# Pair attention on one Trainium2 core: two parts of a short pair turned into one PSUM bank, read by one copy, and one reciprocal for each pair

## The chip, the core and the metric

The kernel runs on one core of a Trainium2 chip. The time is the device time of one launch in microseconds (us). PE is TensorE's matmul unit, PEld its weight load, DVE is VectorE, ACT is ScalarE, POOL is GpSimd and SP is SyncE.

## What is computed

The reference passes 512 tokens of width 1024 through three transformer blocks. Each has gated linear layers and mixers, and each has softmax attention over short sequences. The change touches only those attentions. Cut to what matters, the three are:

```python
# first block: for each of 16 heads, three branches (compressed keys, selected blocks, window)
p_cmp = masked_softmax(q @ k_cmp.T * scale - slope * distance, seen)      # 31 compressed keys
o = g0 * (p_cmp @ v_cmp) + g1 * (softmax(...) @ v_sel) + g2 * (softmax(...) @ v_win)
# second block: sparse heads, and differential heads
o_sparse = softmax(q @ k.T + bias + penalty) @ v
o_diff = (attn_map(q1, k1) - lam * attn_map(q2, k2)) @ v
# third block: six heads with a forgetting term
logits = q @ k.T * scale + (c[q] - c[k]);  o = softmax(causal(logits)) @ v
```

## The kernel before, in words

Matmuls of the linear layers ("dense" below, lines L719 to L721, three products for one block of 128 input features) are interleaved with the attention by `run_lanes`: each engine has one program for each lane, and `paced` fixes by hand the order in which all five engines step through the lanes. An engine works strictly in that order.

The attention lane is `PairAttend`. Its queries come in tiles of 128 tokens, and an item is a pair of parts (two heads, or the two maps of a differential head) for one query tile t and one kind of key. A part has t + 1 blocks of 128 keys, or one block of 31 for the compressed keys. For item i:

- PE computes the scores of both parts (`scores`, L933; in the third block also L939).
- DVE adds the bias and takes the row minimum (`lowest`, L1007), part by part.
- ACT takes the exponential with its row sum (`exponential`, L1040), part by part.
- DVE inverts the two row sums (`invert`, L987) and multiplies the rows by them and by the gate (`share`, L1023; L1017 and L1019 for joined items, whose two parts become one matrix).
- PE transposes the weights, block by block, into the PSUM tile `turn`, which is one bank of 512 columns (`turn`, L950). ACT copies that bank into `probs_t` (`read_turned`, L1053). The bank is single, so the next turn waits for the copy (`turned_read`).
- PE multiplies with the values (`weigh`, L964) into `out_acc`; ACT copies that out at the end of a group (L1066).

The lane is pipelined by slots. In slot s PE does the scores of item s, the turn of part 0 of item s - 3, the weighing of item s - 4, and then the turn of part 1 of item s - 3. A dense step may follow. ACT in that slot does: copy of part 0, exponential of part 0 of item s, copy of part 1, exponential of part 1. DVE does the minima of item s, then the inversion and the multiplication of item s - 1.

There are 138 items: 96 in the first attention (8 head pairs, 4 query tiles, 3 kinds; the two-deep score buffers are `score_sets=2`), 30 in the second (10 sparse and 20 joined) and 12 in the third. I call the items of one head pair in the first attention A0, A1, A2 (t = 0), B0, B1, B2 (t = 1), C0 to C2 and D0 to D2, where kind 0 is the compressed one with 31 keys. In the first attention POOL also builds the bias tables of the next head pair in the meantime.

## Time and profile before

| | |
|---|---|
| median of 3 runs | 3330.89 us (3327.81 to 3335.61) |
| the profiled execution | 3334.52 us, its span 3332.8 us |
| PE busy, over the span | 3032.6 us, 91% |
| ACT, DVE, POOL busy | 35%, 34%, 37% |
| granted PE clock, mean | 0.943 of full speed |
| first attention | about 229 to 493 us of the span |
| second attention | about 1633 to 1790 us |
| third attention | about 2745 to 2826 us |

Busy PE time is the time covered by its matmuls from start to modelled end. Since matmuls are pipelined, what a step costs PE is better read as the time from its first start to the start of the next step. All such intervals below are differences of two start times in the timeline.

### The profile page before, as it was taken

The page shows a single profiled execution, that of the slowest core. Times are in us where ns is not written, and L with a number is a line of the kernel's source. Part 1 is how long each engine was busy: PE and PEld are TensorE (multiplying, and loading weights), DVE is VectorE, ACT ScalarE, POOL GpSimd, SP SyncE. Part 2 cuts the span into 40 slices and gives each one's busy share as a digit, 9 for nine tenths or more (in the row PEclk, how much of TensorE's full clock was granted, in tenths as well). Part 3 has the DMA queues.
Part 4 walks back from the last instruction along what each step waited for, and adds up shares of the span by engine and source line. Part 5 has one row for each costly group of instructions (what it writes and reads, how often), then busy time and mean ns, then how long its engine had stood idle before and what let it go on. Part 6 is the DMA issues. An engine that isn't in the chain of part 4 may idle for free. (4 is left out here: it accounts for less than half of the span.)

```text
span 3332.8 us, 44710 instructions
## 1 busy us (share of the span) xinstructions
PE 3032.6 (91%) x17513; PEld 2486.4 (75%) x17513; DVE 1123.0 (34%) x2511; ACT 1152.6 (35%) x2136; POOL 1240.2 (37%) x599
## 2 busy tenths in 40 slices
PE   4879999998999959999999989999897899989998
PEld 3765557887877757766787989999786756868877
DVE  4116651111132031664353432220364732322210
ACT  3237763222243223343354422221233345423221
POOL 3232214454344412122122535544354422535543
PEclk8889999999999977999899989999898999989999
DMA  6320002232232202012122412223222222413322
GB/s 225 109 63 20 20 15 87 89 101 82 89 108 83 89 26 69 26 45 64 64 78 81 160 58 88 88 88 97 69 79 91 73 69 78 163 63 95 101 88 95
DMA packets 83502, 272.96 MB, mean 82 GB/s; under 512 B 9879, under 2 KB 10135, under 8 KB 83204
## 3 DMA queue, kind: packets, MB, share of 16 engines
q1 hardware_dynamic: 80956, 267.62, 25.3%
q10 hardware_dynamic: 2376, 3.00, 0.3%
q8 instruction: 116, 1.90, 0.2%
q14 instruction: 54, 0.44, 0.0%
HBM read 255.68 MB, written 14.90 MB: 81 GB/s over the span
## 5 line engine op out<-in xcount | busy, mean ns | idle before, releaser
L157 POOL TENSOR_TENSOR weights_lo<-weights_raw,weights_hi 128x1024 fp32r<-128x1024 f32 x415 | 1009.1, 2438 | 1370.5 <-ACT weights_hi L149 1370.3
L149 ACT ACTIVATE weights_hi<-weights_raw 128x1024 fp32r<-128x1024 f32 x415 | 436.8, 1056 | 859.0 <-PE acc L721 347.5
L195 PE MATMUL acc<-h_hi,weights_hi 128*128 128x264 f32 (+1 forms) x1616 | 546.9, 338 | 44.2 <-PEq L87 36.2
L719 PE MATMUL acc<-h_hi,weights_hi 128*128 128x512 f32 (+1 forms) x1336 | 509.1, 381 | 50.4 <-PEq L513 18.9
L196 PE MATMUL acc<-h_lo,weights_hi 128*128 128x264 f32 (+1 forms) x1616 | 545.3, 337 | 0.0
L197 PE MATMUL acc<-h_hi,weights_lo 128*128 128x264 f32 (+1 forms) x1616 | 545.1, 337 | 0.0
L720 PE MATMUL acc<-h_lo,weights_hi 128*128 128x512 f32 (+1 forms) x1336 | 477.6, 358 | 0.0
L721 PE MATMUL acc<-h_hi,weights_lo 128*128 128x512 f32 (+1 forms) x1336 | 476.8, 357 | 0.0
L719 PEld LDWEIGHTS acc<-h_hi,weights_hi 128*128 128x128 f32 x1336 | 262.6, 197 | 139.8 <-issue 108.8
L195 PEld LDWEIGHTS acc<-h_hi,weights_hi 128*128 128x128 f32 x1616 | 307.9, 191 | 76.9 <-issue 46.3
L196 PEld LDWEIGHTS acc<-h_lo,weights_hi 128*128 128x128 f32 x1616 | 308.1, 191 | 30.8
L197 PEld LDWEIGHTS acc<-h_hi,weights_lo 128*128 128x128 f32 x1616 | 307.9, 191 | 30.9
L721 PEld LDWEIGHTS acc<-h_hi,weights_lo 128*128 128x128 f32 x1336 | 262.8, 197 | 33.5
L720 PEld LDWEIGHTS acc<-h_lo,weights_hi 128*128 128x128 f32 x1336 | 263.5, 197 | 28.6 <-issue 0.9
L195 PE MATMUL acc<-hidden_hi,weights_hi 128*128 128x264 f32 (+1 forms) x528 | 170.7, 323 | 15.0 <-PEq L87 15.0
L196 PE MATMUL acc<-hidden_lo,weights_hi 128*128 128x264 f32 (+1 forms) x528 | 170.5, 323 | 0.0
L197 PE MATMUL acc<-hidden_hi,weights_lo 128*128 128x264 f32 (+1 forms) x528 | 170.2, 322 | 0.0
L1053 ACT ACTIVATE probs_t<-turn 31x128 f32<-31x128 f32 (+5 forms) x256 | 99.0, 387 | 156.3 <-PE turn L950 152.7
L1040 ACT ACTIVATE probs<-probs,low 128x31 f32<-128x31 f32 (+5 forms) x276 | 139.2, 505 | 31.1 <-DVE low L1007 30.8
L1148 POOL TENSOR_TENSOR hidden_lo<-full,hidden_hi 128x528 f32 (+3 forms) x44 | 57.7, 1311 | 236.5 <-DVE hidden_hi L1204 236.5
L1194 DVE TENSOR_SCALAR conv<-gate_pad,vec 128x528 f32<-128x528 f32 (+1 forms) x44 | 24.2, 551 | 319.1 <-ACT gate_pad L1177 319.1
L950 PE MATMUL turn<-const,probs 128*128 128x128 f32 (+3 forms) x564 | 111.5, 286 | 20.7 <-ACT probs_t L1053 13.6
(392 smaller groups left out, 4815.4 us busy)
## 6 DMA issues: line engine op xcount, KB each, us to landing
weights_raw<-in_stream SPq DMA_DIRECT2D x415, 512.0 KB, 3.6
weight_ring<-in_w_ada SPq DMA_DIRECT2D x24, 512.0 KB, 12.2
gates<-gate_tiles SPq DMA_DIRECT2D x24, 264.0 KB, 4.4
gate<-gates SPq DMA_DIRECT2D x8, 792.0 KB, 5.8
gates<-gate_tiles SPq DMA_DIRECT2D x24, 256.0 KB, 4.3
gate<-gates SPq DMA_DIRECT2D x8, 768.0 KB, 5.6
flipped<-bias_rows SPq DMA_DIRECT2D x8, 320.0 KB, 4.6
x<-in_x ACTq DMA_DIRECT2D x1, 2048.0 KB, 21.5
```

The source lines that it names most:

```text
L149: act.activation(self.hi[:, at % CUT, :], self.raw[:, at % RAW, :], ACT.Copy).then_inc(self.hi_done, 1)
L157: pool.tensor_tensor(self.lo[:, at % CUT, :], self.raw[:, at % RAW, :], self.hi[:, at % CUT, :].bitcast(F32), ALU.subtract).then_inc(self. ...
L195: pe.matmul(accs[half], w_hi, x_hi[:, cols], start=start, stop=False)
L196: pe.matmul(accs[half], w_hi, x_lo[:, cols], start=False, stop=False)
L197: last = pe.matmul(accs[half], w_lo, x_hi[:, cols], start=False, stop=stop)
L719: pe.matmul(out, left[0], right[0], start=start, stop=False)
L720: pe.matmul(out, left[0], right[1], start=False, stop=False)
L721: return pe.matmul(out, left[1], right[0], start=False, stop=stop)
L950: last = pe.transpose(self.turn[0:kb, b * part.nq:(b + 1) * part.nq], self.probs[0:part.nq, self.place(i, m), c:c + kb], self.k.ident[0:pa ...
L1040: act.activation(rows, rows, ACT.Exp, bias=self.low[0:part.nq, at, :], scale=-1.0, accum_out=self.row_sum[0:part.nq, at, :]).then_inc(self ...
L1053: last = act.activation(to[0:rows, 0:len(full) * part.nq], self.turn[0:rows, 0:len(full) * part.nq], ACT.Copy)
L1148: pool.tensor_tensor(tile_at(hidden.lo, i, n, w), full[:, u], tile_at(hidden.hi, i, n, w).bitcast(F32), ALU.subtract).then_inc(rest_done, 1)
```

## The change

A pair that is not joined, whose parts together fill at most 512 columns and whose blocks are all of one height, is turned at once: the transposes of both parts go one behind the other into the same bank, part 1 in the columns behind part 0, with one semaphore count, and one ACT instruction copies both (its output jumps by 512 columns between the parts). PE then weighs without a second turn behind it. Such pairs are those with one or two blocks: A and B items and all kind 0 items in the first attention (64 of 96), 4 of 30 in the second, 6 of 12 in the third, 74 in all. Longer pairs and joined ones go as before. In all 138 items DVE inverts both row sums in one instruction, which waits for both exponentials.

```diff
+        self.at_once = [not joined and 2 * len(a.blocks) * a.nq <= 512 and len(set(kb for _, kb in a.blocks)) == 1 for a, _, joined in self.items]
+        turns = [1 if joined or once else 2 for (_, _, joined), once in zip(self.items, self.at_once)]
...
         def turn(i, m):
             part, n = self.items[i][m], self.turns_to[i] + m
-            pe.wait_ge(self.weights_ready, n + 1)
+            pe.wait_ge(self.weights_ready, self.weights_to[i + 1] if self.at_once[i] else self.weights_to[i] + m + 1)
             if n >= 1:
 
                 pe.wait_ge(self.turned_read, n)
-            for b, (c, kb) in enumerate(part.blocks):
-                last = pe.transpose(self.turn[0:kb, b * part.nq:(b + 1) * part.nq], self.probs[0:part.nq, self.place(i, m), c:c + kb],
-                                    self.k.ident[0:part.nq, 0:part.nq])
+            for both in range(2 if self.at_once[i] else 1):
+                for b, (c, kb) in enumerate(part.blocks):
+                    col = (both * len(part.blocks) + b) * part.nq
+                    last = pe.transpose(self.turn[0:kb, col:col + part.nq], self.probs[0:part.nq, self.place(i, m + both), c:c + kb],
+                                        self.k.ident[0:part.nq, 0:part.nq])
             last.then_inc(self.turned, 1)
...
         def invert(i):
-            for m in range(2):
-                nq, at = self.items[i][m].nq, self.place(i, m)
-                dve.wait_ge(self.exp_done, 2 * i + m + 1)
-                dve.reciprocal(self.row_inv[0:nq, at, :], self.row_sum[0:nq, at, :]).then_inc(self.row_inverted, 1)
+            nq, at = self.items[i][0].nq, self.place(i, 0)
+            dve.wait_ge(self.exp_done, 2 * i + 2)
+            dve.reciprocal(self.row_inv[0:nq, at:at + 2, 0], self.row_sum[0:nq, at:at + 2, 0]).then_inc(self.row_inverted, 1)
...
             rows = part.blocks[0][1]
+            if self.at_once[i]:
+                cols = len(part.blocks) * part.nq
+                act.activation(self.probs_t[0:rows, 2 * (i % 2):2 * (i % 2) + 2, 0:cols], self.turn[0:rows, 0:2 * cols].rearrange("p (m c) -> p m c", m=2),
+                               ACT.Copy).then_inc(self.turned_read, 1)
+                return
...
-            if turns is not None and not self.items[turns][2]:
+            if turns is not None and self.two_turns(turns):
                 read_turned(turns, 1)
```

On PE, in the first attention in the third head pair, this is the order before, from the scores of a B1 item to those of a C0 item; the turned items are A1 and A2, one block each.

```order
L933 MATMUL scores<-keys_t,q 128x256 x2
L950 MATMUL turn<-const,probs 128x128
L964 MATMUL out_acc<-probs_t,v_cmp 64x128 x2
L950 MATMUL turn<-const,probs 128x128
L719 MATMUL acc<-h_hi,weights_hi 128x512
L720 MATMUL acc<-h_lo,weights_hi 128x512
L721 MATMUL acc<-h_hi,weights_lo 128x512
L933 MATMUL scores<-keys_t,q 128x256 x2
L950 MATMUL turn<-const,probs 128x128
L964 MATMUL out_acc<-probs_t,v_tok 64x128 x2
L950 MATMUL turn<-const,probs 128x128
L933 MATMUL scores<-k_cmp,q 128x31 x2
```

The same place in the changed kernel, whose lines are shifted (L940 for L933, L959 for L950, L973 for L964):

```order
L940 MATMUL scores<-keys_t,q 128x256 x2
L959 MATMUL turn<-const,probs 128x128 x2
L973 MATMUL out_acc<-probs_t,v_cmp 64x128 x2
L719 MATMUL acc<-h_hi,weights_hi 128x512
L720 MATMUL acc<-h_lo,weights_hi 128x512
L721 MATMUL acc<-h_hi,weights_lo 128x512
L940 MATMUL scores<-keys_t,q 128x256 x2
L959 MATMUL turn<-const,probs 128x128 x2
L973 MATMUL out_acc<-probs_t,v_tok 64x128 x2
L940 MATMUL scores<-k_cmp,q 128x31 x2
```

The second transpose moved from behind the weighing to in front of it; nothing else on PE moved, and there are as many matmuls as before.

On ACT, where item A0 is turned, and just before it the last turn of D2 is copied, the order before is this (`probs_t<-turn` is the copy, `q<-out_acc` the output of a group):

```order
L1053 ACTIVATE probs_t<-turn 128x512
L1040 ACTIVATE probs,row_sum<-probs,low 128x128
L1053 ACTIVATE probs_t<-turn 31x128
L1040 ACTIVATE probs,row_sum<-probs,low 128x31
L1053 ACTIVATE probs_t<-turn 31x128
L1040 ACTIVATE probs,row_sum<-probs,low 128x31
L1066 ACTIVATE q<-out_acc 128x128
```

And in the changed kernel, with the two items behind it:

```order
L1066 ACTIVATE probs_t<-turn 128x512
L1048 ACTIVATE probs,row_sum<-probs,low 128x128
L1060 ACTIVATE probs_t<-turn 31x2x128
L1048 ACTIVATE probs,row_sum<-probs,low 128x31 x2
L1079 ACTIVATE q<-out_acc 128x128
L1060 ACTIVATE probs_t<-turn 128x2x128
L1048 ACTIVATE probs,row_sum<-probs,low 128x256 x2
L149 ACTIVATE weights_hi<-weights_raw 128x1024
```

The copy that stood between the two exponentials is gone; one copy of twice the columns stands ahead of both.

## Rows read from the trace of the kernel before

**Rows 1.** Busy us and count of each engine, clock, DMA: first attention

```profile
229.00:493.00 264.00, 236.30 (x1729) 140.80 (x1730) 164.16 (x769) 177.97 (x626) 59.89 (x40) 0.97 0.07 21
```

**Rows 2.** Timeline of PE, third head pair: start, us, instruction, idle before

```profile
303.67 0.41 PE L933 MATMUL scores<-k_cmp,q 64*128 64x31 f32 x4
304.01 0.30 PE L950 MATMUL turn<-const,probs 128*31 128x128 f32 x1
304.24 1.09 PE L964 MATMUL out_acc<-probs_t,v_tok 128*64 128x128 f32 x16
305.26 0.30 PE L950 MATMUL turn<-const,probs 128*31 128x128 f32 x1
305.49 0.70 PE L933 MATMUL scores<-keys_t,q 64*128 64x256 f32 x4
306.12 0.33 PE L950 MATMUL turn<-const,probs 128*128 128x128 f32 x1
306.47 0.43 PE L964 MATMUL out_acc<-probs_t,v_cmp 31*64 31x128 f32 x4
306.91 0.30 PE L950 MATMUL turn<-const,probs 128*128 128x128 f32 x1
306.97 0.48 PE L719 MATMUL acc<-h_hi,weights_hi 128*128 128x512 f32 x1
...
308.48 0.33 PE L950 MATMUL turn<-const,probs 128*128 128x128 f32 x1
308.74 0.44 PE L964 MATMUL out_acc<-probs_t,v_tok 128*64 128x128 f32 x4
309.27 0.30 PE L950 MATMUL turn<-const,probs 128*128 128x128 f32 x1
309.50 0.41 PE L933 MATMUL scores<-k_cmp,q 64*128 64x31 f32 x4
310.03 0.27 PE L950 MATMUL turn<-const,probs 128*31 128x128 f32 x1
310.23 0.44 PE L964 MATMUL out_acc<-probs_t,v_tok 128*64 128x128 f32 x4
310.75 0.27 PE L950 MATMUL turn<-const,probs 128*31 128x128 f32 x1
310.77 0.47 PE L719 MATMUL acc<-h_hi,weights_hi 128*128 128x512 f32 x1
```

**Rows 3.** Timeline of PE, third attention, an item with two blocks

```profile
2770.55 0.44 PE L950 MATMUL turn<-const,probs 128*128 128x128 f32 x2
2770.92 0.44 PE L964 MATMUL out_acc<-probs_t,v_tok 128*64 128x128 f32 x4
2771.55 0.41 PE L950 MATMUL turn<-const,probs 128*128 128x128 f32 x2 [0.20 <-ACT probs_t L1053]
2771.72 0.48 PE L719 MATMUL acc<-h_hi,weights_hi 128*128 128x512 f32 x1
```

**Rows 4.** Timeline of PE, second attention, dense work right behind a weighing

```profile
1650.03 0.45 PE L964 MATMUL out_acc<-probs_t,v_tok 128*64 128x128 f32 x4
1650.41 0.39 PE L719 MATMUL acc<-h_hi,weights_hi 128*128 128x264 f32 x1
```

**Rows 5.** Timeline of PE, two turns with idle time ahead

```profile
241.54 0.39 PE L950 MATMUL turn<-const,probs 128*31 128x128 f32 x1 [1.14 <-ACT probs_t L1053]
...
312.73 0.41 PE L950 MATMUL turn<-const,probs 128*128 128x128 f32 x2 [0.18 <-DVE probs L1023]
```

**Rows 6.** Timeline of ACT: the copy of B0's second part

```profile
312.34 0.25 ACT L1053 ACTIVATE probs_t<-turn 31x128 f32<-31x128 f32 x1
```

**Rows 7.** Timeline of DVE: both multiplications of B1

```profile
309.53 2.35 DVE L1023 TENSOR_SCALAR probs<-probs,row_inv,gates 128x256 f32<-128x256 f32 x2
```

**Rows 8.** Groups by line and shape, first attention: count, busy us, mean ns, idle

```profile
L987 DVE RECIPROCAL row_inv<-row_sum 128x1 f32<-128x1 f32 x192 | 22.7, 152 | 2.5 <-ACT probs L1040 2.3
...
L1053 ACT ACTIVATE probs_t<-turn 128x512 f32<-128x512 f32 x32 | 19.1, 597 | 18.5 <-PE turn L950 18.5
```

More of the change, by code:

```diff
@@ L881, in __init__ @@
         self.last_of = [max(i for i in range(N) if self.of[i][0] == g) for g in range(len(groups))]
-        turns = [1 if joined else 2 for _, _, joined in self.items]
+        self.at_once = [not joined and 2 * len(a.blocks) * a.nq <= 512 and len(set(kb for _, kb in a.blocks)) == 1 for a, _, joined in self.items]
+        turns = [1 if joined or once else 2 for (_, _, joined), once in zip(self.items, self.at_once)]
+        weights = [1 if joined else 2 for _, _, joined in self.items]
+        self.weights_to = [sum(weights[:i]) for i in range(N + 1)]
         self.turns_to = [sum(turns[:i]) for i in range(N + 1)]
@@ L900, in __init__, with two_turns @@
         self.weights = [item[0].nk for item in self.items] + [P] * (self.WEIGH + 1)
+    def two_turns(self, i):
+        return self.turns_to[i + 1] - self.turns_to[i] == 2
     def place(self, i, m):
@@ L1013, in share @@
             inv = [self.row_inv[0:part.nq, self.place(i, m), :] for m, part in ((0, a), (1, b))]
-            dve.wait_ge(self.row_inverted, 2 * i + 2)
+            dve.wait_ge(self.row_inverted, i + 1)
             if joined:
@@ L1070, in act @@
                 exponential(s, 0)
-            if turns is not None and not self.items[turns][2]:
+            if turns is not None and self.two_turns(turns):
                 read_turned(turns, 1)
```

## The prediction, made before the changed kernel ran

> **What bounds the kernel now.** I looked first at the busy shares: PE is busy 91% of the span, no other engine over 37%. Then at the three attention stretches alone. In the first, the busiest beside PE is ACT with 178 of 264 us, then DVE with 164, and PE has 236 [rows 1]. So ACT and DVE could follow a somewhat faster PE, and the question is what each slot costs PE. Busy time does not tell this, because a transpose that is "busy" for 0.30 us lets the next instruction start after 0.06 or after 0.23 us. I therefore read starts in PE's timeline. The reader should see there that a slot is a chain of small steps with little named idle time, yet every step that has to wait for a semaphore begins late. A turn of one block followed by another such step takes 0.23 us (305.26 to 305.49), 0.20 with 31 keys (310.03 to 310.23). One followed by dense work takes 0.06 or 0.02 us (306.91 to 306.97, 310.75 to 310.77) [rows 2]. The second thing to see is a round trip. From the start of part 0's turn to the start of part 1's it is 306.12 to 306.91 = 0.79 us and 308.48 to 309.27 = 0.79 us, with only two short products between them; for two blocks it is 2770.55 to 2771.55 = 1.00 us, and there 0.20 us of it shows as idle, ended by the copy [rows 2, 3]. The one bank has to be copied by ACT before part 1 can go in. Where the weighing is long, as behind D2 (304.24 to 305.26 = 1.02 us), it hides the copy.
>
> **The change, part by part.**
>
> The weighing without a round trip in it. Where nothing is turned behind it, a weighing of one block takes 1650.03 to 1650.41 = 0.38 us [rows 4], against 0.44 to 0.53 us in rows 2 (306.47 to 306.91, 308.74 to 309.27). Four blocks take 1.02, so each further block is (1.02 - 0.38) / 3 = 0.21: two blocks 0.59, three 0.81. No row shows a weighing with scores right behind it; it could be as cheap as 0.38 or pay once more the 0.17 us by which a gated step behind a turn (0.23) exceeds an ungated one (0.06). I take 0.38, because the weighing is followed in rows 2 by a gated turn and there, with 1.02 us for four blocks, no such surcharge is visible. The other end is 0.17 us in each of the 22 slots without dense work, 4 us.
>
> The joint turn. Two transposes in a row take 0.37 us (2770.55 to 2770.92) [rows 3], one takes 0.26 (308.48 to 308.74) [rows 2]: one more costs 0.11. With 31 keys I take 0.23 + 0.11 = 0.34, with two blocks (four transposes) 0.37 + 0.22 = 0.59.
>
> Now slot by slot, turn + weighing + turn before, and joint turn + weighing after. The counts are those of the eight head pairs, whose rows repeat; "dense" says that dense work comes right behind.
> - A0, weighing four blocks: before 0.23 + 1.02 + 0.23 = 1.48, after 0.34 + 1.02 = 1.36. Saves 0.12, three times. With dense behind, the second turn cost only about 0.05 and the slot loses about 0.08, four times. C0 and D0 have the same form with two or three blocks weighed: save 0.12 six times, lose 0.08 nine times. Together 9 x 0.12 - 13 x 0.08 = 0.
> - A1 and A2: before 0.26 + 0.53 + 0.23 = 1.02, after 0.37 + 0.38 = 0.75. Saves 0.27 eight times. With dense 0.35 + 0.44 + 0.06 = 0.85, saves 0.10, eight times. Sum 3.0 us.
> - B0, weighing A2: before 0.20 + 0.52 + 0.02 = 0.74 with dense, after 0.72: 0.1 us over six. The two without dense wait longer for the copy and I give them 0.4 each, 0.8. But B0's first turn has to wait for the copy of A2's second part: the 31-key scores ahead of it last 309.50 to 310.03 = 0.53, against 303.67 to 304.01 = 0.34. After the change the weighing (0.38) and the scores (0.34) lie behind A2's turn (0.37), 1.09 us, over the round trip of 1.00. The 0.19 goes, six times 1.1. Sum 2.0.
> - B1: before as in rows 3, 0.37 + 0.63 + 0.17 = 1.17, after 0.59 + 0.38 = 0.97, eight times 0.20 = 1.6. And the 0.18 us idle ahead of B1's first turn [rows 5]. The row names DVE, but B0's second copy ends 312.34 + 0.25 = 312.59 [rows 6], so that is what it waits for; that copy stood behind an exponential, which stood behind DVE's slow multiplication (309.53 to 311.88) [rows 7]. After the change the copy stands ahead of both exponentials. Five head pairs show this idle time, 0.9 us.
> - B2, weighing two blocks: with dense 1.17 before and 0.59 + 0.59 = 1.18 after, nothing; three times without dense the second turn costs 0.34 and not 0.17: 0.5 us.
> - The very first pair: its second turn sat idle for 1.14 us behind the copy, because ACT was still doing exponentials [rows 5]. That idle time goes: 1.1 us.
>
> First attention: 0 + 3.0 + 2.0 + 2.5 + 0.5 + 1.1 = 9.1 us. The second attention has two A and two B items with PE's time in the same form: about 0.5 for the idle time of its first pair, 0.1, 0.3 and 0: 0.9. The third has three and three: 0.5 + 0.1 + 0.1 + 0.2 + 0 + 0 = 0.9. These four smaller figures are estimates by the same three rows. Sum 10.9 us.
>
> What it costs on the engines behind. The joint copy starts one or two transposes later and has twice the columns. It is hidden by weighing and scores, 0.72 us at the least, as computed for B0; the margin there is only 0.09. ACT itself: in slot A2 it has one copy and two exponentials of 256 columns, and PE needs 0.63 + 0.75 = 1.38 us without dense work. ACT may be behind PE there by a few tenths, and a rounding of weights also falls in this place. B1's joint turn waits for both multiplications. They ended at 311.88, the turn began at 312.73, 0.85 us later; PE will come some 0.5 us earlier by then. I deduct 0 to 3 us for such lateness and take 0.4, because both margins are positive in the rows.
>
> The reciprocals. 138 instructions of about 0.15 us leave DVE [rows 8], 21 us. DVE's multiplications are ready 0.85 us or more before PE wants them, so this is worth nothing on PE's path; if that cover were gone it would be worth up to 0.15 us in an item, and in such items it would reduce the lateness above. The joint one waits for the second exponential; the multiplications waited for that anyway.
>
> The sum: 10.9 - 0.4 = 10.5 us. Against the profiled execution, 3334.5 - 10.5 = 3324.0. That execution lay 3.6 us above the median of the three runs, so the median becomes 3330.9 - 10.5 = 3320.4 us.
>
> The Trainium skill speaks against this part of the change. Perfetto Trace Analysis, section Optimizing Scalar/DVE Operations, says that where ACT or DVE are not saturated but cause bubbles on another engine, breaking instructions up may let work finish sooner; here the instruction is made larger, with ACT at 178 of 264 us. By that rule this would cost time, the second rival below. The rows side with the merger, since the bubble they show is the number of round trips through one bank and not the length of a copy.
>
> **The rivals.**
> 1. Gain given back by ACT and DVE, so that nothing can be measured. For it: the margins 0.09 and 0.85 us, and slots of 1.38 us in which ACT must fit two exponentials. Against it: ACT and DVE have a third of the stretch free. If the surcharge of 0.17 us behind the weighing holds (4 us) and lateness costs 3, then 10.9 - 7 = 4 us remain: 3327.
> 2. The late half, on the slower side. What comes next on the bank waits for the whole joint copy. A 512-column copy takes 0.60 us [rows 8], and it can start only after four transposes. If it were exposed in each of the 74 slots by 0.25 us (an estimate: the copy's added half 0.21, and the added transposes partly), it would cost 18 us against 11 gained: 3338. It decides where exposure is over 11 / 74 = 0.15 us in every slot. Against it: the cover is 0.72 us or more, and 1.6 us with dense work.
> 3. More is gained: the same removed round trip also lets scores and exponentials go earlier, and the remaining waits for the bank in C and D items shrink. Idle times of the kind shown stand before other turns too. I bound it by doubling the two waits priced for B0 and B1, 2 us, and by 0.15 us of DVE lead in 32 short items where it is slowest, 5 us: 3314.
> 4. The change does not do what it says: excluded by the order, which shows the joint turn and copy.
>
> **How the numbers follow.** Forecast (gain of 7 to 14 us) 0.66; rival 1 (gain under 7, about nothing) 0.20; rival 3 (over 14) 0.10; rival 2 0.04. No change means within 0.2%, 6.7 us, about what a measurement here can tell. Faster: forecast and rival 3, 0.76, and a little of rival 1's upper end does not count: 0.76. Same 0.20, slower 0.04. The range runs from rival 3's 3314 to just beyond rival 1, 3328; it leaves out rival 2 and the tails.
>
> **What would show it.** Right: in the same slots, a joint turn then a weighing of 0.38 us and scores or dense work at once; A1 and A2 slots shorter by 0.1 to 0.3 us; the first attention about 9 us shorter, the second and third about 1 us each, everything else as it was; ACT's wait for turns shorter. Wrong: idle time ahead of the joint turns, put down to ACT's copy or DVE's multiplication; a weighing followed by scores that takes 0.55; or a different granted clock in stretches that the change does not touch.

## The result, and the profile after

The changed kernel took 3314.28 us (median of 6 runs, 3309.45 to 3318.38), the kernel before in the same session 3331.89 us (6 runs). The ratio is 0.9943, interval 0.9927 to 0.996: 13 to 24 us less, where 10.5 us less was forecast. Two repeats in later sessions gave 0.9971 (0.9959 to 0.9983) and 0.9947 (0.9928 to 0.9965), so 10 to 19 us is what one should carry. The forecast of 3320.4 us had a range of 3314 to 3328, a gain of 3 to 17 us on the 3330.9 us it started from; the 17.6 us measured here lie just beyond it. The direction and most steps were right. But some two fifths of this saving came from where the prediction had nothing, and one of its terms, B1's, did not come at all.

The profiled execution took 3315.77 us with a span of 3314.1 us, PE's mean granted clock 0.945 (before: span 3332.8 us, 0.943). First the view by windows of the first attention, with the columns of [rows 1]:

```profile
229.00:487.00 258.00, 235.90 (x1728) 140.70 (x1727) 158.41 (x672) 168.57 (x561) 59.85 (x40) 0.95 0.07 21
```

The two windows differ by 6 us because they are cut at whole microseconds; from the first scores to the end of the last weighing it is 262.2 us before and 257.4 after, at a lower clock (0.95 against 0.97), with 97 DVE and 65 ACT instructions fewer. Now PE's timeline in the third head pair, which answers to [rows 2]:

```profile
303.48 0.41 PE L940 MATMUL scores<-k_cmp,q 64*128 64x31 f32 x4
303.82 0.41 PE L959 MATMUL turn<-const,probs 128*31 128x128 f32 x2
304.16 1.09 PE L973 MATMUL out_acc<-probs_t,v_tok 128*64 128x128 f32 x16
305.18 0.70 PE L940 MATMUL scores<-keys_t,q 64*128 64x256 f32 x4
305.82 0.44 PE L959 MATMUL turn<-const,probs 128*128 128x128 f32 x2
306.19 0.44 PE L973 MATMUL out_acc<-probs_t,v_cmp 31*64 31x128 f32 x4
306.55 0.50 PE L719 MATMUL acc<-h_hi,weights_hi 128*128 128x512 f32 x1
...
307.45 0.70 PE L940 MATMUL scores<-keys_t,q 64*128 64x256 f32 x4
308.08 0.44 PE L959 MATMUL turn<-const,probs 128*128 128x128 f32 x2
308.45 0.44 PE L973 MATMUL out_acc<-probs_t,v_tok 128*64 128x128 f32 x4
308.82 0.41 PE L940 MATMUL scores<-k_cmp,q 64*128 64x31 f32 x4
309.16 0.41 PE L959 MATMUL turn<-const,probs 128*31 128x128 f32 x2
309.49 0.44 PE L973 MATMUL out_acc<-probs_t,v_tok 128*64 128x128 f32 x4
309.86 0.50 PE L719 MATMUL acc<-h_hi,weights_hi 128*128 128x512 f32 x1
...
310.75 0.92 PE L940 MATMUL scores<-keys_t,q 64*128 64x384 f32 x4
311.60 0.65 PE L959 MATMUL turn<-const,probs 128*128 128x128 f32 x4
312.69 0.43 PE L973 MATMUL out_acc<-probs_t,v_cmp 31*64 31x128 f32 x4 [0.44 <-ACT q L1079]
313.06 0.50 PE L719 MATMUL acc<-h_hi,weights_hi 128*128 128x512 f32 x1
```

Subtract neighbouring starts. A joint turn takes 308.08 to 308.45 = 0.37 us, with 31 keys 0.34. A weighing of one block takes 308.45 to 308.82 = 0.37 us although gated scores follow it; the surcharge of 0.17 us that was open in the prediction does not exist. From the scores that open one slot to those of the next, the slots in which A1, A2 and B0 are turned went from 2.36, 1.65 and 2.14 us (in the trace of [rows 2]) to 2.27, 1.37 and 1.93. The wrong place is the third from the end: the weighing behind B1's turn of four sat idle for 0.44 us, and from the turn to the weighing it is 1.09 us and not 0.59. ACT's timeline shows why:

```profile
309.82 0.36 ACT L1060 ACTIVATE probs_t<-turn 31x256 f32<-31x256 f32 x1
311.67 0.32 ACT L1048 ACTIVATE probs<-probs,low 128x31 f32<-128x31 f32 x1 [1.49 <-DVE low L1015]
311.89 0.19 ACT L1048 ACTIVATION_READ_ACCUMULATOR probs<-probs,low 128x1 f32 x1
311.99 0.30 ACT L1048 ACTIVATE probs<-probs,low 128x31 f32<-128x31 f32 x1
312.20 0.19 ACT L1048 ACTIVATION_READ_ACCUMULATOR probs<-probs,low 128x1 f32 x1
312.29 0.26 ACT L1079 ACTIVATE q<-out_acc 128x128 f32<-128x128 f32 x1
```

The weighing opens a group, so `out_acc` must have been read. The copy that reads it (L1079) stands behind the exponentials of C0, and these waited for DVE's minima. The same queue was there in the kernel before:

```profile
312.80 0.25 ACT L1066 ACTIVATE q<-out_acc 128x128 f32<-128x128 f32 x1
```

There the copy ended at 313.05 us and the weighing started at 313.19; in the changed kernel the copy ended at 312.55 and the weighing started at 312.69. Both start 0.14 us behind the copy's end. Before, the turn ahead began late, so that only 0.09 us of this showed (312.73 to 313.19 = 0.46 us from turn to weighing, against 0.37 for such a pair of transposes elsewhere). DVE was late, as its timeline in the changed kernel shows, since B1's multiplications took 2.46 us:

```profile
308.87 0.16 DVE L995 RECIPROCAL row_inv<-row_sum 128x2 f32<-128x2 f32 x1
309.07 2.46 DVE L1031 TENSOR_SCALAR probs<-probs,row_inv,gates 128x256 f32<-128x256 f32 x2
311.45 0.17 DVE L1015 CUSTOM_DVE_ANT_0 probs<-scores,alibi_cmp 128x31 f32<-128x31 f32 x1
...
311.86 0.73 DVE L1031 TENSOR_SCALAR probs<-probs,row_inv,gates 128x256 f32<-128x256 f32 x2
```

The same two multiplications took 0.73 us three microseconds later. Beside the slow ones POOL ran this:

```profile
308.68 2.37 POOL L157 TENSOR_TENSOR weights_lo<-weights_raw,weights_hi 128x1024 fp32r<-128x1024 f32 x1 [8.34 <-ACT weights_hi L149]
```

In the whole trace of the changed kernel, each of the 38 multiplications of 128x256 with no POOL instruction beside it took 0.35 to 0.49 us; the eight with this subtraction beside them for over nine tenths of their time took 1.58 to 2.55 us. No run takes the subtraction away, so that it is the cause is likely but not shown.

To size all terms I added up the slots of head pairs 2 to 7 (from the first scores of the second pair to the first scores of the eighth; PE at full clock in both traces) by the item turned in them. "Forecast" is three quarters of the prediction's figure, as these are six of eight pairs:

| us saved in six head pairs | forecast | changed kernel |
|---|---|---|
| A0, C0, D0 and D1 | 0 | 1.4 |
| A1, A2 | 2.3 | 2.3 |
| B0 | 1.5 | 1.6 |
| B1 | 1.9 | -0.2 |
| B2 | 0.4 | 0.5 |
| sum | 6.0 | 5.5 |

These six pairs took 186.88 us before and 181.39 after. In B1's row, the five slots with the wait went from 3.11 to 3.20 us each; the sixth, where nothing waits, gained its 0.2 us as forecast.

### The profile page after: what moved, and what is told of

It is laid out like the page before. It is cut to its first block and busy times, and to the rows that moved or that the text cites. A ratio compares the mean times of both kernels' runs of the same rounds, so it can differ in the third digit from the quotient of the medians.

```text
span 3314.1 us, 44424 instructions
## 1 busy us (share of the span) xinstructions
PE 3021.7 (91%) x17513; PEld 2478.6 (75%) x17513; DVE 1115.1 (34%) x2373; ACT 1141.6 (34%) x2062; POOL 1240.1 (37%) x599
## 5 line engine op out<-in xcount | busy, mean ns | idle before, releaser
L195 PEld LDWEIGHTS acc<-hidden_hi,weights_hi 128*128 128x128 f32 x528 | 100.8, 191 | 22.8 <-issue 15.7
L959 PE MATMUL turn<-const,probs 128*128 128x128 f32 (+3 forms) x564 | 98.1, 284 | 12.3 <-ACT probs_t L1066 11.3
```

The costliest lines, as they stand in the source:

```text
L195: pe.matmul(accs[half], w_hi, x_hi[:, cols], start=start, stop=False)
L959: last = pe.transpose(self.turn[0:kb, col:col + part.nq], self.probs[0:part.nq, self.place(i, m + both), c:c + kb], self.k.ident[0:part.nq ...
```

## Where the rest came from: the clock and a transfer

Outside the attentions, the largest difference between the two first executions lies between the first and the second attention, 1140.2 us before and 1132.8 after. There `BiasTables` turns eight tables on PE, each fetched by SP into one of two buffers (`flipped`). PE's timeline of the kernel before, where the fifth table is turned:

```profile
1594.46 1.53 PE L2329 MATMUL turn<-flipped,const 128*128 128x320 f32 x4 [1.25 <-DMA flipped<-bias_rows]
```

and of the changed kernel:

```profile
1587.38 1.34 PE L2342 MATMUL turn<-flipped,const 128*128 128x320 f32 x4
```

The wait of 1.25 us is gone. Windows of 22 us from just ahead of these turns, before and then changed (the eighth figure, behind POOL's, is the granted clock):

```profile
1590.00:1612.00 22.00, 20.75 (x81) 15.62 (x79) 3.82 (x5) 3.09 (x5) 2.34 (x1) 0.69 0.37 122
```

```profile
1583.00:1605.00 22.00, 21.91 (x120) 16.82 (x119) 5.34 (x7) 5.35 (x10) 3.97 (x2) 1.00 0.37 130
```

PE is busy in both, but did 81 matmuls in the one and 120 in the other: before, PE ran at half clock (1.2 GHz instead of 2.4) for 13.7 us from 1595.5 us on.

The second such place is the second attention itself. It took 154.6 us before, 17.1 of them at half clock, and 148.7 after, 5.3 of them at half clock; less half of that time, both are 146.0 us. So these 5.9 us are clock too. The repeats below had 17.1 and 17.1 us of half clock there before, and 11.5 and 5.4 in the changed kernel. But two kernels with the joint turn (B1 in two halves, and two copies) had 17.4 us each, with no wait of over 0.47 us for a table. What this stretch follows is not shown.

Half clock is all over this program: in the records of granted clock it adds up to 382.2 us before and 365.0 after. While PE is busy, a microsecond at half clock does about half a microsecond's work (81 matmuls against 120 above), so span less half of that time is a rough measure of the work itself. I call it the levelled span: 3141.7 us before, 3131.6 after.

## The experiments

**The kernel before, again,** unchanged (twice).

> The kernel before once more, unchanged. Two theories share the 17.6 us. Slots: the changed slots alone are worth about 5 us in the first attention and 2 in the others; the other 10 or so are TensorE clock, since the changed kernel spent less time at half clock around 1595 to 1650 us of the span. Chance: that clock difference is luck of the two profiled executions. If chance, this profile may show the half clock around 1595 us gone, and its time within 0.1% of the others all the same. If it belongs to the kernel, the half-clock stretches of about 14 us at 1595 us and of about 17 us at 1633 us are here again. Ratio 1.000 in both cases.

> The kernel before a third time. Theory: span less half of the half-clock time 3141 to 3143 us again; the 1.25 us for which TensorE waits for the fifth table's rows may come out anywhere between 0.6 and 1.3 us with the transfer's own time, and the half clock of 13.7 us behind it is there if the wait is 1.2 us or more, as in three executions, and not if it is 1.0 or less. Rival (the stretch of 13.7 us at 1595 us belongs to the kernel before whatever the wait): there at any wait.

**The changed kernel, again,** unchanged (twice).

> The changed kernel itself once more. Theory (the gain over what the slots give is TensorE's clock around 1590 to 1650 us, and belongs to the kernel and not to a single execution): the half-clock stretches come again at 1617.8 us (6.8 us long) and 1768 us, none at 1590 to 1600 us, and the time is 3314.3 plus or minus 3. Rival (the clock's pattern differs from one execution to the next): a half-clock stretch of some 13.7 us at 1590 to 1600 us, and a span of 3320 us.

> The changed kernel a third time. Theory (the change saves 10 to 12 us of work, and what a session measures beyond or below it is how long TensorE ran at half clock): span less half of its half-clock time 3130 to 3132 us as in the first two executions (3131.6 and 3130.4), against 3142 before; the half-clock time may be anything from 350 to 382 us, the span accordingly 3305 to 3322. Rival (the changed kernel belongs to a lower half-clock time, and all of the 18 us is its own): half-clock time again 365 plus or minus 3 us and the time 3314 plus or minus 2, 14 us or more below the kernel before.

| execution | us, ratio to before | span | half clock | levelled span |
|---|---|---|---|---|
| before, first | | 3332.8 | 382.2 | 3141.7 |
| before, second | 3330.03, 0.9999 (0.9987 to 1.0011) | 3330.0 | 375.4 | 3142.2 |
| before, third | 3328.86, 0.9999 (0.9987 to 1.0012) | 3325.4 | 361.7 | 3144.5 |
| changed, first | 3314.28, 0.9943 (0.9927 to 0.996) | 3314.1 | 365.0 | 3131.6 |
| changed, second | 3316.15, 0.9971 (0.9959 to 0.9983) | 3312.9 | 365.1 | 3130.4 |
| changed, third | 3309.54, 0.9947 (0.9928 to 0.9965) | 3308.1 | 351.6 | 3132.3 |

The mean levelled span falls by 3142.8 - 3131.4 = 11.4 us, with 2 to 3 us between executions of one kernel. The stretch behind the fifth table's turn came again in both repeats of the kernel before, for 13.7 and 6.8 us, and in none of the changed kernel's. The mean half-clock time falls by 12.5 us, from 373.1 to 360.6, worth 6.3. Within one kernel it varies by 14 to 20 us from one execution to the next, so three of each can't size this part well. Against the rival of the last expectation the changed kernel's half-clock time was not again 365 but 351.6 us.

**The reciprocal alone,** joined, in the kernel before:

```diff
-            for m in range(2):
-                nq, at = self.items[i][m].nq, self.place(i, m)
-                dve.wait_ge(self.exp_done, 2 * i + m + 1)
-                dve.reciprocal(self.row_inv[0:nq, at, :], self.row_sum[0:nq, at, :]).then_inc(self.row_inverted, 1)
+            nq, at = self.items[i][0].nq, self.place(i, 0)
+            dve.wait_ge(self.exp_done, 2 * i + 2)
+            dve.reciprocal(self.row_inv[0:nq, at:at + 2, 0], self.row_sum[0:nq, at:at + 2, 0]).then_inc(self.row_inverted, 1)
```

> The joint reciprocal alone, everywhere; turns as before. Prediction's step: nothing, because the multiplications are ready 0.85 us or more before PE wants them (ratio 1.000, within 0.001). Rival: the DVE chain behind B1 (multiplications slowed to 1.2 us each) sets the start of the weighing there, and then one reciprocal less on DVE is worth 0.1 us in five head pairs, 0.5 us, still within the noise; over 3 us would mean that DVE holds PE back in many items.

3330.04 us, ratio 0.9996 (0.9985 to 1.0008). Head pairs 2 to 7 took 186.83 us against 186.88 before.

**The joint turn alone,** the reverse of that edit in the changed kernel.

> The changed kernel with the two reciprocals of an item apart again, so the joint turn and copy alone. Theory (the reciprocal lies beside PE's path): the first attention stays at 258.3 plus or minus 0.5 us and the time at that of the changed kernel, 3314 to 3317. Rival (the shorter DVE chain made part of the gain that the joint turn got): the slots in which DVE is slow grow by up to 0.15 us each, 3318 to 3322.

3319.99 us, ratio 0.9973 (0.9963 to 0.9983). The time is nearer to the rival's, the trace is not: head pairs 2 to 7 took 181.37 us against 181.39 in the changed kernel. The reciprocal is worth nothing on PE's path in either direction. The levelled span was 3127.3 us here, 3 us below the changed kernel's lowest with the same slots, so that measure is good to some 5 us and no better.

**The joint turn in the first attention only,** and **in the second and third only** (both with the joint reciprocal). The edit is a flag in one line, set to False for the other attentions:

```diff
-        self.at_once = [not joined and 2 * len(a.blocks) * a.nq <= 512
+        self.at_once = [once and not joined and 2 * len(a.blocks) * a.nq <= 512
```

> The joint turn only in the first attention, the joint reciprocal everywhere. Slots theory: 5 to 6 us from the first attention. If the clock part comes from how the first attention shifts what follows, 15 us or more (ratio 0.9955 or less); if it comes from the second attention's own start, 5 to 7 us (ratio 0.998 to 0.9985).

> The joint turn only in the second and third attention, the joint reciprocal everywhere. Slots theory: about 2 us if the clock part does not come with it (ratio 0.9994), 8 to 12 us if the removed idle time at the start of the second attention is what brings the clock up sooner (ratio 0.9965 to 0.9975).

First only: 3318.77 us, 0.996 (0.9947 to 0.9973); head pairs 2 to 7 in 181.40 us. Late only: 3325.89 us, 0.9986 (0.9976 to 0.9996); the third attention in 78.12 us against 79.13 before, which are the 0.9 us of the prediction and 0.1 more. First only, whose ratio means 9 to 18 us, came nearer in time to the expectation for the clock than to the 5 to 7 us of the slots; by levelled spans (3136.8 and 3141.2 us) the two are worth 6.0 and 1.6 us, close to the slots' figures.

**ScalarE's output copy earlier.** In the changed kernel, the group's output is copied right behind the turned copy of the slot of its weighing:

```diff
-            done = s - self.WEIGH - 1
-            if done >= 0 and self.of[done][2]:
+            done = s - self.WEIGH
+            if turns is not None:
+                read_turned(turns, 0)
+            if 0 <= done < N and self.of[done][2]:
...
-            if turns is not None:
-                read_turned(turns, 0)
```

> The changed kernel, with ScalarE's copy of the group output moved from the slot behind the weighing of D0 (behind the exponentials of C0) to right behind the turned copy of the same slot. Theory (B1's slot lost its gain to a chain that reaches back from the weighing of B0 over the output copy to VectorE): the weighing of B0 no longer waits 0.44 us for L1079 in five head pairs, B1's slot falls from 3.20 to about 2.75 us in each of them, the first attention from 258.5 to some 256.3 us, and the time by 2.0 to 2.5 us below the changed kernel's 3314.3: 3312. Rival (ScalarE's copy, now ahead of the exponentials, waits for a weighing of one to three blocks and holds the exponentials back): the weighing still waits, for the exponentials or for VectorE's multiplications, and the time is 3314 to 3318.

3312.45 us, ratio 0.9962 (0.9948 to 0.9976), beside 0.9971 for the changed kernel in the same session. The intervals overlap; the trace decides. PE's timeline at the place of the 0.44 us:

```profile
307.24 0.92 PE L940 MATMUL scores<-keys_t,q 64*128 64x384 f32 x4
308.08 0.66 PE L959 MATMUL turn<-const,probs 128*128 128x128 f32 x4
308.67 0.43 PE L973 MATMUL out_acc<-probs_t,v_cmp 31*64 31x128 f32 x4
309.03 0.50 PE L719 MATMUL acc<-h_hi,weights_hi 128*128 128x512 f32 x1
```

and ACT's, where the output copy (L1081) now stands ahead of the exponentials that still wait for DVE:

```profile
306.30 0.36 ACT L1060 ACTIVATE probs_t<-turn 31x256 f32<-31x256 f32 x1
306.57 0.25 ACT L1081 ACTIVATE q<-out_acc 128x128 f32<-128x128 f32 x1
308.15 0.32 ACT L1048 ACTIVATE probs<-probs,low 128x31 f32<-128x31 f32 x1 [1.33 <-DVE low L1015]
```

Turn to weighing is 0.59 us, as the prediction had it, and B1's slot 2.69 us against 3.19 (3.11 before). Head pairs 2 to 7 took 178.86 us, 2.5 less than in the changed kernel, and B1's line of the table becomes 2.3 us saved where 1.9 were forecast. So the chain over the output copy is shown to be what ate that term.

**B1 in two halves again** (`at_once` false for the eight B1 items), the rest as in the changed kernel.

> The changed kernel, where in the first attention the eight B1 items are turned in two halves as before. Theory (the joint turn gained nothing in them, since the weighing of B0 then stands waiting for ScalarE's output copy): their slots go from 3.20 to 3.1 to 3.3 us, the first attention stays within 1 us of 258.4, the time within 1.5 us of the changed kernel's. Rival (my own step in the prediction, 2.5 us for B1): the first attention 2.5 us longer, 260.9.

3318.07 us, ratio 0.9966 (0.9953 to 0.998). B1's slot was 3.36 to 3.38 us against 3.19, head pairs 2 to 7 took 182.45 us: 1.1 us more in six pairs, 1.4 in eight. My theory was too strong. The weighing waits there too, 0.65 us by the trace, but the joint turn does save its 0.18 us. The slot is slower than the 3.11 us of the kernel before, with the same two turns. My reading is that the earlier steps have become faster and PE arrives sooner at a wait that ends at ACT's time; this is argued from the trace and has no run of its own.

**The joint turn with two copies,** one right behind the other, one count.

```diff
-                act.activation(self.probs_t[0:rows, 2 * (i % 2):2 * (i % 2) + 2, 0:cols], self.turn[0:rows, 0:2 * cols].rearrange("p (m c) -> p m c", m=2),
-                               ACT.Copy).then_inc(self.turned_read, 1)
+                for both in range(2):
+                    last = act.activation(self.probs_t[0:rows, 2 * (i % 2) + both, 0:cols], self.turn[0:rows, both * cols:(both + 1) * cols], ACT.Copy)
+                last.then_inc(self.turned_read, 1)
```

> The changed kernel with the joint turn, but ScalarE copies its two halves with two instructions one right behind the other, and counts once, behind the second. Theory (what is gained is PE's round trip between the two turns; how many instructions ScalarE has for the copy matters only where PE waits for it): at most 0.1 us more in each of the five B1 slots that already wait, the first attention 258.3 to 259.5, the time within 2 us of the changed kernel's. Rival (the one instruction is what gains): each copy costs ScalarE some 0.2 us more in 74 slots, the first attention grows by 4 us or more, 3319 to 3322.

3314.7 us, ratio 0.9957 (0.9944 to 0.997). Head pairs 2 to 7 took 181.64 us, 0.25 more than with one instruction. Two copies of 128x256 take 0.64 us together, the single one of 128x512 0.58. The gain belongs to PE's program, with one round trip through the bank in place of two.

**The tables' transfers one slot earlier,** with three buffers, in the kernel before:

```diff
-            if head >= 2:
-                sp.wait_ge(self.turned, head - 1)
+            if head >= 3:
+                sp.wait_ge(self.turned, head - 2)
...
-            sp.dma_start(self.flipped[:, head % 2, :], src).then_inc(self.table_in[head % 2], 16)
-            yield
+            sp.dma_start(self.flipped[:, head % 3, :], src).then_inc(self.table_in[head % 3], 16)
+            if head >= 1:
+                yield
```

> The kernel before, with three buffers for the tables' flipped rows in place of two and each of their transfers issued one slot earlier, so that TensorE does not wait for them. Theory (TensorE's halved clock from 1595.5 us on for 13.7 us follows the 1.25 us for which it waited for the transfer of the fifth table): the waits of turn<-flipped for the transfer, 4.6 us in all, go to under 1 us, the half clock at 1595 us is gone, and the time falls by 6.8 us for the clock and up to 4 us for the waits: 3320 (3317 to 3324). Rival 1 (the clock is halved there for another reason): the half clock stays and only the waits go, 3326 to 3328. Rival 2 (what matters is the total time of idle PE before the second attention's start): the stretch moves to 1625 to 1635 us and is longer, no change of over 3 us.

3322.48 us (11 runs), ratio 0.9989 (0.998 to 0.9998), the median 5.5 us below that of the kernel before in its session, by the interval 1 to 7 us less. The levelled span was 3141.6 us against the mean of 3142.8. No turn of a table waits for its transfer, and the window shows no half clock:

```profile
1590.00:1612.00 22.00, 22.00 (x119) 16.93 (x118) 5.35 (x7) 6.01 (x10) 4.74 (x2) 1.00 0.29 92
```

**The fifth table late,** fetched twice in a row (SP waits for the first transfer), in the changed kernel and in the kernel before, and **the sixth late** in the changed kernel:

```diff
+            if head == 4:
+                sp.dma_start(self.flipped[:, 2, :], src).then_inc(self.first_in, 16)
+                sp.wait_ge(self.first_in, 16)
```

> The changed kernel, with the flipped rows of the fifth table fetched twice, the second time after the first has landed, so that TensorE waits for them at about 1587 us as the kernel before did at 1594 us (that one transfer more is 0.33 MB). Theory (a wait of over a microsecond there brings the halved clock): TensorE waits 1 to 4 us ahead of that table's turn, a half-clock stretch of some 13.7 us follows within a few us, and the time is 3314.3 plus the wait plus 6.8: 3322 to 3325. Rival (the clock does not answer to this wait): the time rises by the wait alone, 3315 to 3318, and the half-clock stretches stay as they were.

> The kernel before with the flipped rows of the fifth table fetched twice, so that TensorE's wait there is 1.25 us plus some 3 us. Theory (a wait of over a microsecond brings the half clock): a half-clock stretch begins within 2 us of that wait's end; its length is open, 13.7 us as in the kernel before or 3.4 us as in the changed kernel with the same edit; the time rises by 3 us and the difference of the stretches. Rival (the stretch has nothing to do with the wait): it begins at 1595.5 us as before, wherever the wait ends.

> The changed kernel with the sixth table's rows fetched twice, so that TensorE waits some 3 us there and not at the fifth. Theory (the wait brings the half clock): the stretch of 3.4 us or more moves to that wait, some 6 us later than with the fifth table; the wait is about 3 us and the span less half of the half-clock time rises by it, to 3134 to 3136. Rival (the half clock came by chance at the fifth): no stretch begins within 3 us of the wait's end.

Changed kernel, fifth late: 3322.0 us, 0.9985 (0.9975 to 0.9995), about 6 us above the changed kernel in its session. The time came as expected, the stretch did not: 3.4 us of half clock from 1589.6 us on, and not 13.7. The wait of 3.1 us and half of that stretch make 4.8. Before, fifth late: 3332.54 us, 1.0013 (1.0001 to 1.0025). Its stretch began at 1594.6 us, 2.2 us ahead of the wait's end and 0.3 to 1.4 us from where it began in the kernel before (1594.9 to 1596.0), so this run does not part the theory from its rival. Sixth late: 3314.05 us, 0.9954 (0.9938 to 0.997), where the sixth turn waited only 0.18 us, so the edit did not make the wait it was meant to. But the second turn waited 1.20 us there, on a transfer that the edit does not touch. PE's rows for these waits, in this order:

```profile
1590.13 2.50 PE L2346 MATMUL turn<-flipped,const 128*128 128x320 f32 x4 [3.11 <-DMA flipped<-bias_rows]
```

```profile
1596.76 2.50 PE L2333 MATMUL turn<-flipped,const 128*128 128x320 f32 x4 [4.57 <-DMA flipped<-bias_rows]
```

```profile
1566.10 1.34 PE L2346 MATMUL turn<-flipped,const 128*128 128x320 f32 x4 [1.20 <-DMA flipped<-bias_rows]
```

All profiled executions with such a wait, over all kernels here (half clock that begins within 4 us of the wait's end):

| longest table waits, us | half clock behind it, us |
|---|---|
| 1.25, 1.33, 1.24 (before, before again, late only) | 13.7 each |
| 1.12 (before, third) | 6.8 |
| 4.57 (before, fifth late) | 6.8, begun within the wait |
| 3.11 (changed, fifth late) | 3.4, begun within the wait |
| 1.20 (changed, sixth late) | 3.4 |
| 0.99 (reciprocal alone), 0.94 | none |
| 0.96 twice (changed again; changed, fifth late) | 3.4 once, none once |
| 0.76 and less (in all the others) | none |

Each of the seven table waits of 1.12 us or more had half clock with it, and of the shorter ones only one had. With the two runs that moved the wait (tables earlier: stretch gone; changed kernel, fifth late: stretch there), that ties the stretch to the wait at this place. It is no rule for other waits. In the kernel before, two waits of PE for ACT stand in the same region, with no half clock in them or within 4 us behind them:

```profile
1569.64 1.07 PE L816 MATMUL sums<-sq,const 128*24 128x264 f32 x4 [1.32 <-ACT sq L804]
...
1578.10 1.07 PE L816 MATMUL sums<-sq,const 128*24 128x264 f32 x4 [1.33 <-ACT sq L804]
```

In that whole execution PE was idle for 1.1 to 2.0 us, at full clock, 21 times; half clock began within or up to 4 us behind 10 of them. That a longer wait brings a longer stretch is refuted: the 4.57 us brought 6.8 and the 1.25 us 13.7.

**Both edits together** in the changed kernel, the earlier output copy and the earlier tables.

> The changed kernel with both edits: ScalarE's output copy right behind the turned copy, and three buffers and earlier transfers for the tables' rows. Theory: the output copy is worth the 2.5 us of slots and the 2 to 4 us of first pair and clock that it gave alone; the tables' transfers have only 0.4 us of waiting left to remove, so they add 0 to 1 us, unless a half-clock stretch goes with them: 3309 to 3313, and a span of 3306 to 3309. Rival (the earlier transfers are worth as much here as in the kernel before, 5 us): 3306 or less.

3313.17 us, ratio 0.9953 (0.994 to 0.9966). Head pairs 2 to 7 in 178.86 us and a levelled span of 3124.3 us, the lowest of all, but with 382.2 us of half clock in that execution, so that its span of 3315.4 us missed the expected 3306 to 3309. Levelled spans of kernels with the changed kernel's work scatter from 3127.3 (joint turn alone) to 3132.3 us, so 3 to 8 us are gained by this measure, and by its time it is not told apart from the changed kernel. I would keep both edits, on the evidence of slots and waits.

## Why the prediction was right in most steps and wrong in the number

Two steps failed. Inside the sum it was B1's: the prediction took a wait for gone that only moved on by one instruction. What carried the time out of its range was "everything else as it was", a term put at nothing without a reason: about 6.3 us of clock and 1.4 us of waits for tables came on top.

The sum of the work, 10.5 us, looks as if it held beside the 11.4 us of the levelled spans. That is in part luck. At equal half clock the first attention, from the first scores to the end of the last weighing, took 264.3 us before (third execution, 23.9 us of half clock) and 257.4 in the changed kernel (first execution, 23.8), 6.9 us less where 9.1 were forecast. The third gave 0.9 us, the second 0 to 0.7, so the attentions gave about 8 us and not 10.5. The 11.4 also hold the 1.4 us of table waits, which the prediction did not have; the 1 to 2 us that are left lie within the scatter of that measure. Step by step:

- *The weighing without a round trip, the joint turn:* right to 0.01 us (0.37, 0.59, 0.81 and 1.02 us for one to four blocks; 0.37, 0.34 and 0.59 for the turns). The value taken, no surcharge, was right.
- *A1 and A2, B0, B2:* right, 4.3 us in six pairs against 4.1.
- *A0, C0, D0 = 0:* too low by 1.4 us in six pairs, D1 with them. The prices were right: 0.12 us saved without dense work, 0.07 to 0.09 lost with it. But in three pairs the C0 slot saved 0.19 us instead, since its turn had waited for the copy of B2's second part (the line below) and no longer did; by B0's step the prediction could have listed this too. These are 0.8 of the 1.4. The same kind of wait ahead of D1's turn gave 0.3 (from the scores of D1's slot to its turn 0.51 us before, 0.42 after). The rest is that these six pairs have fewer slots with dense work than all eight.

```profile
379.60 0.27 PE L950 MATMUL turn<-const,probs 128*31 128x128 f32 x1 [0.22 <-ACT probs_t L1053]
```

- *"After the change the copy stands ahead of both exponentials. Five head pairs show this idle time, 0.9 us", and the 1.6 us beside it:* the failed step of the sum. The idle time ahead of B1's turn did go. But the prediction asked only what the turn waits for, not what the weighing right behind it waits for. Since PE came sooner, it met the output copy, 0.44 us in the same five pairs, behind the same slow multiplications. A removed wait moved by one instruction: each of these slots grew by 0.09 us where a gain of 0.38 was forecast. With the output copy moved ahead, B1 gave 2.3 us in six pairs.
- *The first pair, 1.1 us:* the slot of its A0 fell from 3.05 to 1.93 us, as forecast, though 0.30 of the 1.14 us idle are left ahead of the joint turn, now for DVE. The whole pair took 35.48 us before and 36.94 after, with more half clock in it (the stretch at 228.6 us lasted 23.9 us, against 20.5 at 226.7), so this term can't be read from the two first executions. At about equal half clock in the pair (23 to 24.4 us) it took 37.3 to 37.7 us in six executions with the turns apart and 36.6 to 36.9 in six with the joint turn, some 0.8 us less.
- *Second and third attention, 0.9 each:* right for the third, which fell from 79.1 to 78.2 us at equal half clock (3.4 us). For the second it is open. At 17.1 to 17.4 us of half clock it fell from 154.6 to 153.9 us (B1 in halves, two copies); at 13.3 to 13.6 us it took 153.6 with the turns apart (tables earlier) and 153.3 to 153.4 with the joint turn (output copy earlier, both edits), and also 153.4 in the first-only kernel, where the second attention is as before.
- *Lateness 0.4 us and "everything else as it was":* the second half failed, and it is this step that put the time out of its range. Here are about 6 us of clock and 1.4 us of waits for tables (1.9 us before, 0.5 after, means of three, and part of the 11.4). How much of the clock belongs to the change stays open, since it varies as much between executions of one kernel. The prediction named a different clock elsewhere as what would make it wrong, and gave it no price and no place in the range.
- *Rivals.* The late half was wrong everywhere: a joint copy of 128x512 took 591 ns, and from 250 us on no wait of PE names the joint copy. What PE waits for is, in the view of waits, the copies of the long pairs (at the same 29 places as before and as long, though before four of them named DVE), and the output copy:

```profile
PE turn L959 <- ACT probs_t L1066: 11.1, 29, 0.8
```

```profile
PE out_acc L973 <- ACT q L1079: 2.2, 5, 0.4
```

The first rival named the right engines, but its price came out at 0.5 us a pair in one item, and it was smaller than what came on top.

The rule of the Trainium skill that the prediction cited against the change (Perfetto Trace Analysis, Optimizing Scalar/DVE Operations) did not decide: splitting the copy again in the two-copies kernel cost 0.25 us in six pairs and gained nothing. On the clock, the Trainium skill, TensorE: Matmul & The Clock Gate, section HAM oscillation, says that a wait for a DMA can throttle PE, so that the next matmuls start cold. The traces agree with the direction in the seven table waits from 1.12 us up; the two waits for ACT of 1.32 and 1.33 us show that not every wait of that length does it.

What stays open: why the fifth table's transfer came in time in the changed kernel. It was issued 1.4 us behind the start of the fourth table's turn in both (1588.37 behind 1586.94, and 1582.44 behind 1581.02). The longest of the eight transfers took 6.4 us to landing before and 5.2 after, and no experiment touched what that depends on. Open too: how long a half-clock stretch becomes, which differed between executions of one kernel, and what the half clock in the second attention follows.

## What to carry to other kernels

When two steps share one buffer, price a removed round trip by start-to-start times of the steps around it; these held here to 0.01 us. Then walk one instruction further on the waiting engine: PE arrives earlier at whatever the next instruction waits for, and that wait must be read from its own producer's queue. And where the kernel before shows stretches of half clock behind short waits far from the change, put their worth (here 7 us for one of 13.7 us) into the range, in both directions.

## What the runs showed of the hardware

- PE's granted clock fell to half in, or right behind, table waits of 1.12 to 1.33 us, for 3.4, 6.8 or 13.7 us. It stayed full at waits of 1.32 and 1.33 us for ACT in the same region.
- Executions of one kernel differ by up to 20 us in their half-clock time (361.7 to 382.2 us), while the same six head pairs took 186.87, 186.88 and 186.81 us. Slots are a finer measure than the run's time by a factor of a hundred.
- DVE's two multiplications of 128x256 took 2.46 us beside a POOL subtraction of 128x1024 and 0.73 us with nothing on POOL.
